# Low parts of the weight chunks: from two halves on VectorE and GpSimd to one instruction on VectorE

## The reference

```python
def swiglu_ffn(x, w_gu, w_down):
    g, u = jnp.split(x @ w_gu, 2, axis=-1)
    return (jax.nn.silu(g) * u) @ w_down
...
def hybrid_layer(x, ...):
    h = rmsnorm(x, norm_mix)
    z = h @ w_in
    ...                                     # split z in q, k, v, gates; att and hm from them
    hm = rmsnorm(hm, m_head_norm.reshape(M_HEADS, M_V_DIM)).reshape(B, S, M_V_W)
    hm = hm * jax.nn.sigmoid(o_m)
    g_a, g_m = jnp.split(gates, 2, axis=-1)
    mixed = jax.nn.sigmoid(g_a) * (att @ w_att_branch) + jax.nn.sigmoid(g_m) * (hm @ w_m_branch)
    x = x + mixed @ w_out
    u = jax.nn.relu(rmsnorm(x, norm_ffn) @ w_ff1)
    return x + (u * u) @ w_ff2
```

## Time and profile before

| | |
|---|---|
| median of 3 runs | 1538.04 us (1537.49 to 1538.27) |
| profiled execution | 1542.43 us, span 1540.6 us |
| TensorE busy | 1418.3 us, 92% |
| VectorE busy | 824.9 us, 54%, 1190 instructions |
| ScalarE busy | 686.2 us, 45% |
| GpSimd busy | 670.2 us, 44%, of which `w_lo` 660.1 |
| granted TensorE clock, mean | 0.964 |

### The profile page before, as it was taken

The page is one execution under the profiler, slowest core; times in us unless marked ns, Lnnn a source line. Parts: engine busy times, 40 slices in busy tenths (PEclk is TensorE's granted clock), DMA queues, the critical chain, the costliest instruction groups (busy, mean ns, idle before and its releaser), DMA issues.

```text
span 1540.6 us, 28612 instructions
## 1 busy us (share of the span) xinstructions
PE 1418.3 (92%) x11701; PEld 1371.4 (89%) x11701; DVE 824.9 (54%) x1190; ACT 686.2 (45%) x827; POOL 670.2 (44%) x216
## 2 busy tenths in 40 slices
PE   5758989999899999999899898999999999799998
PEld 5548989999889899999789898999998899799998
DVE  7985574434633574335584655753247655756421
ACT  4744453333565353334555443443345544434432
POOL 0113535556344345665233342466543324246653
PEclk9978999999999999999899999999999999999999
DMA  5085647666343446665244354457744434446662
GB/s 120 11 136 161 185 114 196 184 179 182 112 164 110 135 136 179 180 191 165 82 139 135 102 173 137 145 183 191 189 139 138 137 109 165 137 137 190 189 180 70
DMA packets 340447, 227.52 MB, mean 148 GB/s; under 512 B 21672, under 2 KB 335248, under 8 KB 340128
## 3 DMA queue, kind: packets, MB, share of 16 engines
q1 hardware_dynamic: 340352, 226.14, 51.3%
HBM read 222.70 MB, written 1.05 MB: 145 GB/s over the span
## 4 chain that ended last, share of the span: by engine, by line
issue 61%; POOL 25%; PE 11%; SPq 1%; DMA 1%; POOLq 1%; ACT 0%; ACTq 0%; DVE 0%
POOL w_lo L379 25%; PE PS L396 4%; PE PS L398 4%; PE PS L397 4%; DMA d_diag<-in_ssm_d_dram 1%; POOLq L334 0%; SPq L1288 0%; POOLq L377 0%; SPq L1292 0%; POOL d_diag L1583 0%; SPq L1285 0%; ACT out_sb L2395 0%; PE PS L2388 0%; SPq L1286 0%; SPq L1294 0%
## 5 line engine op out<-in xcount | busy, mean ns | idle before, releaser
L379 POOL TENSOR_TENSOR w_lo<-raw,w_hi 128x1024 fp32r<-128x1024 f32 x208 | 660.1, 3175 | 815.6 <-ACT w_hi L372 815.6
L396 PE MATMUL PS<-x_hi,w_hi 128*128 128x256 f32 x1952 | 570.0, 292 | 38.5 <-DVE w_lo L379 17.0
L397 PE MATMUL PS<-x_lo,w_hi 128*128 128x256 f32 x1952 | 563.4, 289 | 0.0
L398 PE MATMUL PS<-x_hi,w_lo 128*128 128x256 f32 x1952 | 563.2, 289 | 0.0
L372 ACT ACTIVATE w_hi<-raw 128x2048 fp32r<-128x2048 f32 x208 | 396.6, 1907 | 219.1 <-PE PS L398 219.1
L379 DVE TENSOR_TENSOR w_lo<-raw,w_hi 128x1024 fp32r<-128x1024 f32 x208 | 282.3, 1357 | 276.1 <-ACT w_hi L372 276.0
L396 PEld LDWEIGHTS PS<-x_hi,w_hi 128*128 128x128 f32 x1952 | 386.4, 198 | 44.2 <-issue 33.2
L397 PEld LDWEIGHTS PS<-x_lo,w_hi 128*128 128x128 f32 x1952 | 386.7, 198 | 0.1
L398 PEld LDWEIGHTS PS<-x_hi,w_lo 128*128 128x128 f32 x1952 | 385.9, 198 | 0.0
L396 PE MATMUL PS<-hid_hi,w_hi 128*128 128x256 f32 x1248 | 354.8, 284 | 9.5 <-DVE hid_lo L670 9.4
L397 PE MATMUL PS<-hid_lo,w_hi 128*128 128x256 f32 x1248 | 353.1, 283 | 0.0
(11 more groups left out here) (336 smaller groups left out, 1295.7 us busy)
## 6 DMA issues: line engine op xcount, KB each, us to landing
raw<-in_w_ff_dram SPq DMA_DIRECT2D x128, 512.0 KB, 4.6
raw<-in_ffn_w_gu_dram SPq DMA_DIRECT2D x88, 512.0 KB, 5.0
raw<-in_w_in_dram SPq DMA_DIRECT2D x68, 512.0 KB, 4.7
raw<-in_sb_w_qkv_dram SPq DMA_DIRECT2D x24, 512.0 KB, 4.6
raw<-in_ffn_w_down_dram SPq DMA_DIRECT2D x20, 512.0 KB, 4.8
raw<-in_ssm_w_glu_dram SPq DMA_DIRECT2D x16, 512.0 KB, 5.4
raw<-in_w_out_dram SPq DMA_DIRECT2D x16, 512.0 KB, 4.6
raw<-in_ssm_w_out_dram SPq DMA_DIRECT2D x8, 512.0 KB, 4.5
```

Of the source, the lines that this page charges most:

```text
L379: e.tensor_tensor(w_lo[s][:, cols], raw[s][:, cols], w_hi[s][:, cols].bitcast(F32), ALU.subtract).then_inc(done, 1)
L396: nc.tensor.matmul(dst, lhs_hi, r_hi, start=start, stop=False, skip_group_check=True)
L397: nc.tensor.matmul(dst, lhs_hi, r_lo, start=False, stop=False, skip_group_check=True)
L398: return nc.tensor.matmul(dst, lhs_lo, r_hi, start=False, stop=stop, skip_group_check=True)
```

## The change

`split_lo` now issues one instruction on VectorE for all 2048 columns. GpSimd's loop over the chunks is gone, so nothing follows its setup. The two semaphores become one, `lo_done`: TensorE waits for one before a chunk, SyncE for one before a load.

```diff
         def load_chunk(eng, g, idx, k):
...
             if not isinstance(j, int) or j >= RING:
-                eng.wait_ge(lo_dve, j - (RING - 1))
-                eng.wait_ge(lo_pool, j - (RING - 1))
+                eng.wait_ge(lo_done, j - (RING - 1))
...
-        def split_lo(eng, c, idx, k, half, done):
+        def split_lo(dve, c, idx, k):
             s = (c + k) % RING
-            e = nc.vector if half == 0 else nc.gpsimd
-            eng.wait_ge(hi_done, idx + (c + 1))
-            cols = slice(half * HALF, (half + 1) * HALF)
-            e.tensor_tensor(w_lo[s][:, cols], raw[s][:, cols], w_hi[s][:, cols].bitcast(F32),
-                              ALU.subtract).then_inc(done, 1)
+            dve.wait_ge(hi_done, idx + (c + 1))
+            nc.vector.tensor_tensor(w_lo[s][:, :], raw[s][:, :], w_hi[s][:, :].bitcast(F32), ALU.subtract).then_inc(lo_done, 1)
...
         def weights_split(pe, chunk):
-            pe.wait_ge(lo_dve, chunk + 1)
-            pe.wait_ge(lo_pool, chunk + 1)
+            pe.wait_ge(lo_done, chunk + 1)
...
             s5_pool(pool)
 
-            chunk_loop(pool, n_chunks, 0, 0, lambda idx, k, turn: split_lo(pool, 0, idx, k, 1, lo_pool))
-
```

More of the change, by code:

```diff
@@ L34 @@
 CH = 2048
-HALF = CH // 2
 SG, SH, SP, SL = 64, 16, 64, 8
@@ L316, in stack @@
         act_step, dve_step = S("act_step"), S("dve_step")
-        hi_done, lo_dve, lo_pool = S("hi_done"), S("lo_dve"), S("lo_pool")
+        hi_done, lo_done = S("hi_done"), S("lo_done")
         chunk_done = S("chunk_done")
@@ L618, in body @@
                 if not isinstance(idx, int) or g.c0 + idx + RING < n_chunks:
-                    split_lo(dve, g.c0 + RING, idx, k, 0, lo_dve)
+                    split_lo(dve, g.c0 + RING, idx, k)
             if only is not None or g.shape == "kt4":
@@ L628, in resid_lo @@
             if g.c0 + idx + RING < n_chunks:
-                split_lo(dve, g.c0 + RING, idx, idx % RING, 0, lo_dve)
+                split_lo(dve, g.c0 + RING, idx, idx % RING)
         def tile_ready(dve, g, t):
@@ L1762, in s5_vector @@
             V.tensor_copy(*state_places(3, 1, 0)).then_inc(st_dve, 1)
-            split_lo(dve, 0, 0, 0, 0, lo_dve)
+            split_lo(dve, 0, 0, 0)
             for half in range(2):
@@ L1770, in s5_vector @@
             for j in range(1, RING):
-                split_lo(dve, 0, j, j, 0, lo_dve)
+                split_lo(dve, 0, j, j)
         ztile = sb("ztile", [P, 10, T], "hl", 16 * 4 * T)
```

## The result

The changed kernel takes 1502.41 us, the median of 4 runs (1501.68 to 1504.35), against 1538.15 for the kernel before beside it. The ratio is 0.9765, with a 95% interval of 0.9748 to 0.9782: 2.35% faster. Forecast were 1506.0 and a range of 1497 to 1519. The profiled execution took 1501.68 with a span of 1499.9, 40.7 less than the span before; the profiled execution of before was one of its slower ones, so its span overstates the gain by some 5 us.

What follows compares the result with a forecast made beforehand. TensorE's pace bounds the weight loops, so only its waits between them on VectorE's chains, stalled behind GpSimd, can be won. Waits −22.4 and clock −9.6 make −32.0 us: from 1538.04 to 1506.0, range 1497 to 1519.

Steps and rivals of the forecast that it cites:

- What bounds it: TensorE sets the pace in the weight loops; only its waits between them, for VectorE's chains, can be won.
- What is added: VectorE's low part takes 2.29 us for 2048 columns in place of 1.23, +1.07 each when uncontended.
- the mix: Hybrid layer's mix: two stalls, 2.9 us, less one low part of 1.07; −1.9 us.
- What is taken away: Every stall of VectorE behind GpSimd, summed by place: −11.35 us a hybrid layer, −22.4 us in all.
- the fourth rival: Long rows aren't GpSimd's doing and each low part adds 1.07 us to its chain: 1557 us; chance 0.06.
- The norm: Norm before the feed-forward part: −0.8 us, with some 3.9 of TensorE's 4.80 us wait staying.
- The clock: Half clock at 1.2 GHz behind four waits a layer partly regained: 4.8 us a layer, −9.6 us.
- heads: mLSTM heads: three of four stalls on the path, 1.9 us each against +1.07; −3.4 us a layer.
- first feed-forward chunk: TensorE's 2.29 us wait for GpSimd's half shortens, as VectorE alone finishes earlier; −1.15 us a layer.
- The first, the clock stays: Rival: only the waits go and the clock stays as it is: 1515.6 us; chance 0.18.
- The third, gaps refill: Rival: successors behind each stall take half the gain, 1527 us, or all, 1538; chance 0.12.
- The second: Rival: more comes back, all clock falls of a layer plus slack that stalls had eaten: 1498 us; chance 0.14.

Runs made afterwards that it cites:

- the run with 1024 columns: The changed kernel with VectorE making the low part of only the left 1024 columns after the first three chunks, right halves keeping old values; 1483.01 us.
- The decoys: The changed kernel with needless GpSimd work beside it per chunk: a two-operand subtraction 1600.11 us, three memsets 1503.93, a one-operand copy 1515.06.
- the run with the gates alone: The kernel before, with three chunks of each hybrid layer made whole on VectorE, so the stalls of the gates' chain go; 1528.09 us, ratio 0.9914.
- the hold: The changed kernel with TensorE held at the gates by GpSimd memsets, five in the first hybrid layer, six in the second; 1509.69 us against 1501.50 without.

## Why the prediction was right, point by point

**What bounds it.** Right. The loops gave nothing, the places between them all of it.

**What is added.** The duration, 2.29, was right to the hundredth. My count of its price ahead of the run with 1024 columns, 9 us, was too low: that run shows 19. At the penalties and the norms the prediction had set the price against a stall and only the count forgot it. In the mix the prediction was wrong too: the price is 2.1, since two low parts stand there and not one, and the stalls are then worth 3.9 and not 2.9. That the mix still came out at −1.8 against −1.9 is luck, two errors of 1 us that cancel.

**What is taken away.** Every term for a layer came within 0.5 us, and the waits together at −24.2 against −22.4. The decoys show the cause: GpSimd's reading beside VectorE's two-input work, not its semaphore and not its late halves. Against the fourth rival I had written that the long rows read both operands; that holds for the rows I had picked, but casts with one operand were stalled as well, up to 1940 ns for 293, and a write by GpSimd is enough for them. The Trainium skill ("SBUF — State Buffer", Who interferes with whom) says that a VectorE instruction with two SBUF inputs contends with a GpSimd instruction that reads SBUF and not with one that only writes it, and that whichever issues first blocks the other. The decoys agree: 1976 ns beside reading, 161 beside writing. The ports that it names are in no trace.

**The norm.** The step was wrong in its reading. I took the 4.80 of the earlier trace rows for the end of the norm's chain and said that 3.9 would stay as such. What stays is TensorE waiting for the low part of the second feed-forward chunk, which the pair of chunks needs and VectorE makes behind the sums of squares; moving that one instruction took it all away. The row had named it: it says w_lo.

**The clock.** The term that was sized too low: −9.6 forecast for the two layers, −8.5 and −5.5 = −14.0 in the traces, about −11.5 by the medians. I counted half where over 1 us of the wait would stay (heads, first feed-forward chunk), and it came back whole at both; and in the first layer a fall at 850.8 that I had not counted went too. Behind it is the same mistake twice, one fall tied to one wait: the run with the gates alone shows waits of 1.90 that bring none once the wait at the gates is gone, and a wait of 2.44 that brings one where the same wait had brought none. The prediction also says that four waits had half clock behind them; it was five, the norm's too, and that one stays. In the second layer the counterpart of the fall at 850.8 stays, and a stretch of half clock stands at 1200 us that was not there before, +1.5, with no wait near it. What sets off these falls stays open.

**The rivals.** The first, the clock stays, is out by the stretches that are at 2.4 GHz now, by the gates' run and by the hold. The fourth, the long rows are not GpSimd's doing, is out by the decoys. The third, gaps refill, didn't happen: the waits gave back as much as forecast or more. The second was half right: the clock gave back more than its forecast, and the measured time lies between the two.

## What to carry to other kernels

Before half of an elementwise step goes to GpSimd, look for one form of VectorE instruction with two durations, the long one ending with GpSimd's; where VectorE's work reads two operands from SBUF the help can cost more than it brings. Price such a change by the chains that TensorE waits for, not by busy time (VectorE went from 54% to 61% busy and the kernel became 2.35% faster), and take the name in a wait at its word before looking for a deeper cause. A long instruction that only fills a buffer for later belongs where its engine waits anyway.

## What the runs showed of the hardware that I had not expected

A memset by GpSimd leaves VectorE's two-input product alone (161 ns) but holds up a float32 cast from SBUF to SBUF (from 293 ns to a median of 702). GpSimd's copy of 1008 columns takes 1.03 us against 2.4 for a subtraction of 1024, and holds a product up as well (648 ns). The clock stayed at 2.4 GHz behind a hold of 1.40 us and behind a wait of 1.90 elsewhere, and fell behind a hold of 2.46; behind one and the same wait of 2.4 us in the mix it fell in one of four cases (two traces, two layers each).
